# Four edits to the order of work: filter taps one panel earlier, a shift of weight slots earlier, a loop over attention heads on TensorE, and a VectorE block ahead of two others

## The reference

```python
z = short_conv(h @ w_in + b_in, conv_w, conv_b)      # width 3, per channel
x0, x1, v = jnp.split(z, 3, axis=-1); s = v * x1
h = act(feat @ w1 + b1); h = act(h @ w2 + b2); h = act(h @ w3 + b3)   # act = sin(freq * a)
g = (h @ w_out) * exp(-t * abs(decay)); g = g / sum(abs(g))
y = irfft(rfft(s) * rfft(g)) + s * skip              # long convolution
x = x + (silu(x @ w_gate) * (x @ w_up)) @ w_down
# second block: 4 heads of GLA, forward and backward, each with its own
# low-rank gate, q, k, v, two gates of the output; then the pooling branch
```

## Time and profile before

| | |
|---|---|
| time, three executions | 2385.44, 2385.83 (median), 2386.75 us |
| profiled execution: its own time, its span | 2386.75 us, 2384.7 us |
| PE busy | 2337.4 us (98% of the span) |
| DVE, POOL, ACT busy | 1274.5, 831.2, 669.1 us |
| mean granted PE clock | 0.990 of full speed |
| chain that ended last | PE 75%, DVE 3%, POOL 1%, ACT 1% |

### The profile page before, as it was taken

One profiled execution on the slowest core, in us unless ns is written; L12 is line 12 of the kernel. 1 busy time (PEld: TensorE's weight loads), 2 busy tenths in 40 slices (PEclk: granted clock), 3 DMA queues, 4 the chain that ended last, 5 costly groups with the idle time before them and its releaser, 6 DMA issues.

```text
span 2384.7 us, 28896 instructions
## 1 busy us (share of the span) xinstructions
PE 2337.4 (98%) x11640; PEld 1883.7 (79%) x11640; DVE 1274.5 (53%) x1287; ACT 669.1 (28%) x787; POOL 831.2 (35%) x495
## 2 busy tenths in 40 slices
PE   8999999899999999999999999999999999999997
PEld 6766773588888878888887989888897877778886
DVE  7966445642775465544287826272733134542576
ACT  5343324522001122211134626362622011110112
POOL 2312211132337976543242212112222333333253
PEclk9999999999999999999997999999999999999998
DMA  4233339512332111131112111020215221132433
GB/s 169 59 119 106 114 120 375 195 45 88 119 111 71 45 53 54 53 106 45 53 62 106 45 42 56 29 71 28 80 36 194 100 68 58 58 130 64 158 98 115
DMA packets 88189, 220.51 MB, mean 92 GB/s; under 512 B 24583, under 2 KB 36681, under 8 KB 87819
## 3 DMA queue, kind: packets, MB, share of 16 engines
q1 hardware_dynamic: 74890, 182.16, 22.8%
q10 hardware_dynamic: 7712, 26.22, 2.9%
q0 software_dynamic: 5472, 10.50, 1.5%
HBM read 171.65 MB, written 42.47 MB: 90 GB/s over the span
## 4 chain that ended last, share of the span: by engine, by line
PE 75%; DVE 3%; POOL 1%; ACT 1%; issue 0%; ACTq 0%; DMA 0%; DVEq 0%; POOLq 0%
PE ps L1534 46%; PE ps L1827 6%; PE ps L1841 5%; PE ps L636 5%; PE ps L1930 4%; DVE T L2465 2%; PE ps L1912 1%; PE ps L683 1%; PE ps L703 1%; PE ps L665 1%; PE ps L704 1%; PE ps L702 1%; PE ps L1802 0%; POOL Ht L1373 0%; DVE X L2857 0%; PE ps L593 0%
## 5 line engine op out<-in xcount | busy, mean ns | idle before, releaser
L1534 PE MATMUL ps<-H,whi 128*128 128x512 f32 x3264 | 886.1, 393 | 3.9 <-DVE H L2534 3.9
L1534 PEld LDWEIGHTS ps<-H,whi 128*128 128x128 f32 x3264 | 613.4, 189 | 148.9 <-issue 22.9
L1336 POOL CAST whi<-wraw 128x1024 fp32r<-128x1024 f32 x150 | 166.6, 1111 | 1296.3 <-PE ps L1534 617.6
L1534 PE MATMUL ps<-H,wlo 128*128 128x512 f32 x1632 | 504.1, 390 | 0.0
L1338 POOL TENSOR_TENSOR wlo<-wraw,whi 128x1024 fp32r<-128x1024 f32 x154 | 403.2, 2618 | 45.0 <-ACT whi L779 32.9
L1534 PEld LDWEIGHTS ps<-H,wlo 128*128 128x128 f32 x1632 | 307.7, 189 | 64.9
L1534 PE MATMUL ps<-A,whi 128*128 128x512 f32 x960 | 257.2, 390 | 2.6 <-DVE A L2928 2.6
L1534 PEld LDWEIGHTS ps<-A,whi 128*128 128x128 f32 x960 | 179.8, 188 | 41.0 <-DVE A L2928 3.5
L1534 PE MATMUL ps<-A,wlo 128*128 128x512 f32 x480 | 147.8, 389 | 0.0
L1827 PE MATMUL ps<-A,whi 128*128 128x512 f32 x512 | 136.8, 389 | 0.0
L1827 PEld LDWEIGHTS ps<-A,whi 128*128 128x128 f32 x512 | 96.1, 188 | 20.0
(11 more groups left out here) (458 smaller groups left out, 3350.2 us busy)
## 6 DMA issues: line engine op xcount, KB each, us to landing
wraw<-in_panels SPq DMA_DIRECT2D x189, 512.0 KB, 3.6
g<-gsp SPq DMA_DIRECT2D x16, 512.0 KB, 3.7
gr<-g SPq DMA_DIRECT2D x16, 512.0 KB, 9.9
bs<-s SPq DMA_DIRECT2D x16, 512.0 KB, 10.2
mw<-in_modp SPq DMA_DIRECT2D x16, 512.0 KB, 3.5
YB<-yi POOLq DMA_DIRECT2D x14, 512.0 KB, 9.3
s<-sa SPq DMA_DIRECT2D x8, 512.0 KB, 2.6
s<-gsp SPq DMA_DIRECT2D x8, 512.0 KB, 3.1
```

What stands on the lines that cost most here:

```text
L1336: nc.gpsimd.tensor_copy(whi[:, s, :, :], wraw[:, s, :, :]).then_inc(hi_made, 1)
L1534: last = mm(p[:, c * step:(c + 1) * step], w[:, ws, k, :], operand(act, a, k, c * step, step), start=(q == 0 and w is whi and a == 0), sto ...
```

## The change

The first edit moves the values and the spreads of every two taps one panel forward in `ZTAP`: values follow panels 5 to 12 (before 6 to 13), spreads panels 6 to 13 (before 7 to 14). The order of ACT, DVE and SP follows from the same functions.

The second edit sets `Q_JUMP` to item 51 (before 54). By the table, the slots of items 50 to 56 are then 3, 2, 3, 0, 1, 2, 3 (before 3, 0, 1, 2, 1, 2, 3), and the items that had these slots before them (`QPREV`) are 46, 49, 50, 47, 48, 51, 52 (before 46, 47, 48, 49, 52, 53, 50). No engine's order changes by it; `high(51)` and `high(52)` wait for other items.

The third edit puts heads 1 to 3 on PE into a loop of three trips. The fourth brings the DVE work on panels 2 and 3 into one loop with that on panels 0 and 1, which sets the sine argument of `mlp1` ahead of the reading of panel 2.

```diff
 def tap_values_of(n):
 
+    return range(2 * (n - 5), 2 * (n - 4)) if 5 <= n < 13 else ()
+
+
+def tap_spreads_of(n):
+
     return range(2 * (n - 6), 2 * (n - 5)) if 6 <= n < 14 else ()
-
-
-def tap_spreads_of(n):
-
-    return range(2 * (n - 7), 2 * (n - 6)) if 7 <= n < 15 else ()
...
-Q_JUMP = item("f", S_END - 1)
+Q_JUMP = item("d", S_END - 4, 1)
...
-            for h in range(1, HEADS):
+            with pe.Fori(1, HEADS) as h:
                 heads_pe(pe, h, free, panel_mm)
...
-            first_z(0)
-            first_z(1)
-            for h in range(2):
-                s_conv(h, 0, h, (zp, zq)[h])
-            first_z(2)
-            argument_turns(1)
-            argument_rest(1)
-            first_z(3)
-            for h in range(2):
-                s_conv(2 + h, 1, h, (zp, zq)[h])
+            for i in range(2):
+                first_z(2 * i)
+                first_z(2 * i + 1)
+                for h in range(2):
+                    s_conv(2 * i + h, i, h, (zp, zq)[h])
+                if i == 0:
+                    argument_turns(1)
+                    argument_rest(1)
```

## The result

The changed kernel takes 2402.45 us (median of four, 2401.38 to 2403.57) against 2386.29 us for the kernel before in the same session (four, 2385.44 to 2387.05). The ratio is 1.0067 (95% interval 1.0054 to 1.0080), that is +16.2 us. The direction was forecast, the size was not: +9.0 us and at most 2398.5 had been predicted. All the shares and instruction counts of TensorE are those of before; its busy time has grown from 2337.4 us to 2348.1 with the same 11640 matmuls, and the mean granted clock has fallen from 0.990 to 0.986, which is 0.4% of the span or some 10 us.

The account below looks back on a forecast made before the run. TensorE, busy 98% of the span, was taken to bound the kernel by its matmuls and their clock. Terms 3.9 + 5.0 + 0.1 = +9.0 us on the profiled 2386.75 gave 2395.8, as median 2394.8; range 2390.5 to 2398.5.

Parts of the forecast that it names:

- First stage: Argument ahead of panel 2 and taps a panel earlier: 7.3 us wait plus 1.7 clock less 5.1 given back, +3.9 us.
- 7.0 for 7.3: First stage, panel 4: TensorE was to wait 7.3 us (bounds 4.6 and 8.4) for VectorE to read panel 2.
- 2.1 for 1.7: First stage, behind the panel 4 wait: the slower clock was to cost 1.7 us.
- The 5.1: First stage: the old 3.2 us wait behind panel 7 and its slow clock were to go, 5.1 us (bounds 0 and 5.1).
- Slots: Outputs `d12`: the cast of item 52 waits for item 50, delaying the third output job, +5.0 us (2.5 to 5.3).
- 3.5 for 3.7: `d12`: TensorE was to wait 3.7 us (bounds 2.9 and 4.0) at the third output job for `ps2`.
- the clock's 1.7: `d12`: 1.7 us (0 to 1.7) for the slower clock behind the wait, as charged to each new wait above 3 us.
- tile 15: After `d12`: the 0.38 us wait for a `wlo` was to go, since item 55 can be cast earlier, -0.4 us.
- Heads: Heads 1 to 3 as a loop on TensorE: jump, register instructions and branches were to cost +0.1 us, bounds 0 and 2.
- The only row on it is an existing loop on TensorE: Heads: 768 matmuls with branches in 174.09 us, 0.2267 each as outside a loop, so branches were taken to show no cost.
- Only two are above 3 us: TensorE's waits in the kernel before: only 5.7 us for a DMA and 3.2 us in the first stage were counted.

Follow-up runs that it names:

- e3: Kernel before with the fourth edit alone (sine argument's block ahead of the reading of panel 2, taps as before): +3.8 us (1.7 to 6.0).
- e2: Kernel before with the second edit alone (`Q_JUMP` at item 51): +5.0 us (2.9 to 7.2).
- e9: Kernel before with the second edit, and in tile 14 both silus on ScalarE ahead of the cast of item 52: -1.0 us (-3.1 to 1.2).
- e1: Kernel before with the third edit alone (heads 1 to 3 in a loop on TensorE, its start not set): +7.6 us (5.0 to 10.3).
- e6: Kernel before with the heads loop, its first instruction placed 26 instructions before a fetch block's end: +4.8 us (2.6 to 6.9) against before.
- e5: Kernel before with the heads loop, its first instruction placed at the start of a 256-instruction fetch block: +1.7 us (-0.5 to 4.1) against before.
- e7: Kernel before with the heads loop, its first instruction placed 56 instructions before a fetch block's end: +0.2 us (-1.9 to 2.4) against before.
- e8: Kernel before with the heads loop, its jump announced by `hint_back_edge=True` and no start slot set: +0.5 us (-1.7 to 2.6) against before.
- e10: Kernel before with VectorE reading panel 7 and the values of taps 2 and 3 ahead of the sums of taps 0 and 1: -4.3 us (-6.4 to -2.1).

## Why the prediction was wrong

- *First stage, +3.9 us.* Right: 4.0 measured. The mechanism is right in each part, but that the sum is so close is partly luck: the wait was 0.3 too long (7.0 for 7.3) and the clock 0.4 too small (2.1 for 1.7). The 5.1 were given back in full, and e3 shows that VectorE's order alone does it.
- *Slots, +5.0 us.* The mechanism was right in each link (e2, e9). Of the terms the wait was 3.5 for 3.7, and the clock's 1.7 was too small: 5.99 us at half clock are 3.0. The term was taken from the two waits of the earlier trace rows, as a fixed price, and it is none. Measured 5.9, with 0.7 and not 0.4 given back in tile 15.
- *Heads, +0.1 us, bounds 0 and 2.* This is the step that failed: 6.7 us in the trace, 7.6 (5.0 to 10.3) alone. "The only row on it is an existing loop on TensorE" was the error. The 768 matmuls of the earlier trace rows are two loops of two trips, with a body of 192 matmuls; their jumps back cost nothing, and the trace of before has only 3 packets of instructions in these 174 us, where 768 matmuls written out would need 6. The prediction carried this over to a body of some 780 matmuls, which in the changed kernel was fetched again at each jump back. It counted what a trip executes, registers and a branch, and not what a jump has to bring: instructions. It also bounded the cost by the length of a short instruction, when nothing in the rows measured a fetch. The hole itself is small (0.2 to 1.2 us); most of the 6.7 us is the clock behind it.
- The Trainium skill speaks against this edit, and the prediction did not weigh it: Runtime: NRT & Kernel Launch, "Instruction fetch mechanics", says that a taken branch whose target is outside the fetched blocks has to fetch it first, and that a block is 256 instructions. The changed kernel, e1 and e6 agree with it. Whether a loop of this length still lies in the fetched blocks is what it leaves open here: in e5, e7 and e8 nothing was fetched for a jump back over some 1590 instructions.
- *A reading.* "Only two are above 3 us" is wrong: before has five waits of TensorE above 3 us (5.7, 4.4, 4.1, 3.9 and 3.2). No edit touches the three that were missed, and they are no term of the sum.
- *The sum.* 3.9 + 5.0 + 0.1 = 9.0 against 4.0 + 5.9 + 6.7 = 16.6. Of the 7.6 us that were missing, 6.6 are the heads.

## What to carry to other kernels

Before a written-out stretch is put into a loop, ask whether each jump back has to fetch instructions again, and look for it in the trace of the loop: packets of the instruction queue in the second trip, and an idle time put down to "issue" shortly behind the jump. Here another place of the start, or a hint, made the same loop free within 2 us or so (e5, e7, e8). When an instruction gets a later thing to wait for, price what is queued behind it on its engine, and move that ahead (e9, e10). And an engine at 98% busy can pay for a small hole a second time by its clock, as in the heads, so small holes are worth a look as well as long waits.

## What the runs showed of the hardware

- A hole's length does not set what the clock takes. In the changed kernel trip 2 lost 2.65 us with a hole of 0.31 us in L598, trip 3 lost 4.06 with one of 0.21 us, while the hole of 0.51 us ahead of L636 in the same trip left the next 240 matmuls at 29.05 us, as in before. L593 and L598 are matmuls on 16 rows; L636 is on 128. Whether this is the reason was not tried.
- After the waits of 7.0 and 3.5 us the clock was at 0.50 for 3.96 and 5.99 us: the shorter wait had the longer slow stretch.
- A VectorE instruction with a single input (L2530) took 2.71 us beside GpSimd's subtraction and 0.69 us alone.
- TensorE can hold a loop of some 1590 instructions through three trips: e5, e7 and e8 have no instruction packet in trips 2 and 3. The same body in e1 and e6 was fetched again in each trip (15 packets of 16 KB from 1560 to 1800 us).
- After a jump back that fetches, the packets came 3.1 to 3.6 us apart in the changed kernel, and TensorE went on 1.2 to 1.7 us after the awaited one had landed (six holes, in the changed kernel, e1 and e6).
